# Attention on one Trainium2 core: in each unit, the value products of the previous unit before the first probability transposes instead of behind them

## What is computed

```python
def one_block(args):            # MLA, one block of 128 queries
    ...
    s = jnp.einsum('bqhd,bkhd->bhqk', qi, k).astype(jnp.float32) * scale
    p = masked_softmax(s, kpos[None, :] <= qpos[:, None])
    return jnp.einsum('bhqk,bkhd->bqhd', p.astype(v.dtype), v)
...
    # NSA: three such softmaxes per block, with a bias from the distance, gated and added
    out = gi[..., 0:1] * o_cmp + gi[..., 1:2] * o_slc + gi[..., 2:3] * o_win
```

## Time and profile before

| what | value |
|---|---|
| median of 3 runs | 3,002.99 us (2,997.59 to 3,006.72) |
| the profiled execution | 2,997.87 us, its span 2,996.1 us |
| the attention sweep in it | about 363 to 820 us from the start |
| TensorE, VectorE, ScalarE busy over the whole span | 90%, 38%, 20% |
| DMA | mean 190 GB/s |

### The profile page before, as it was taken

How to read it: one execution, slowest core, us unless ns; L and a number is a source line. 1 busy time by engine, 2 the same in 40 slices (tenths; PEclk the granted TensorE clock), 3 DMA queues, 4 the chain that set the end, 5 groups by cost and what they waited for, 6 DMA issues and landing times.

```text
span 2996.1 us, 41353 instructions
## 1 busy us (share of the span) xinstructions
PE 2693.9 (90%) x12024; PEld 1334.8 (45%) x12025; DVE 1128.5 (38%) x2931; ACT 587.6 (20%) x1583; POOL 219.9 (7%) x187
## 2 busy tenths in 40 slices
PE   6999789999879974999999899999999999899895
PEld 3555466666545641344444343443333344344332
DVE  2676566767636662222222122222222222222221
ACT  1222255555524320001001010010001001000000
POOL 0000000000001111100000101011110100100110
PEclk9999799999989976999999999999999999999998
DMA  8322753030031208767556877587877777755880
GB/s 295 104 63 55 165 152 87 9 95 15 16 99 50 71 36 315 280 224 291 179 185 235 316 284 268 193 317 264 336 294 268 263 264 253 283 191 186 296 297 15
DMA packets 294261, 570.03 MB, mean 190 GB/s; under 512 B 78606, under 2 KB 117262, under 8 KB 273688
## 3 DMA queue, kind: packets, MB, share of 16 engines
q1 hardware_dynamic: 255309, 530.10, 49.5%
q0 software_dynamic: 21152, 38.52, 5.6%
q10 hardware_dynamic: 17707, 0.22, 0.3%
HBM read 542.62 MB, written 69.88 MB: 204 GB/s over the span
## 4 chain that ended last, share of the span: by engine, by line
PE 48%; DMA 6%; issue 3%; DVE 2%; ACTq 1%; ACT 1%; POOL 0%; POOLq 0%; DVEq 0%; SPq 0%
PE ps L1899 27%; PE ps L1991 17%; DMA out<-ys_e,dst 4%; PE ps L2007 2%; DMA wg<-in_w_gate_up 1%; DMA xg<-d_h,src 1%; DVE gu L1801 1%; PE ps L1872 1%; PE ps L1877 1%; ACTq L1614 0%; DVE ys_e L1845 0%; DVE gg L1804 0%; ACT aT L1719 0%; POOL out L1681 0%; DVE ys_e L1843 0%
## 5 line engine op out<-in xcount | busy, mean ns | idle before, releaser
L1899 PE MATMUL ps<-wg,xT_e 128*64 128x512 f32 (+2 forms) x4032 | 1031.0, 599 | 39.2 <-issue 28.2
L1899 PEld LDWEIGHTS ps<-wg,xT_e 128*64 128x64 f32 (+2 forms) x4032 | 390.5, 146 | 649.3 <-issue 649.3
L1991 PE MATMUL ps<-w_rows,aT 128*128 128x512 f32 x1152 | 518.0, 604 | 30.9 <-ACT xT_e L1699 18.6
L1801 DVE TENSOR_TENSOR gu<-ps,bias 64x512 f32<-64x512 f32 (+2 forms) x252 | 173.6, 689 | 587.9 <-PE ps L1899 552.9
L1991 PEld LDWEIGHTS ps<-w_rows,aT 128*128 128x128 f32 x1152 | 217.8, 194 | 288.1 <-issue 288.1
L1741 ACT ACTIVATE ss<-gg 128x256 f32<-128x256 f32 x146 | 60.8, 416 | 1379.8 <-issue 774.1
L1845 DVE TENSOR_SCALAR ys_e<-ps,dst 128x1024 f32<-128x1024 f32 x36 | 46.2, 1284 | 533.8 <-PE ps L1991 533.8
L1681 POOL DMA_INDIRECT out<-ys_e,dst x64 | 101.9, 1592 | 1342.6 <-DVE ys_e L1845 883.7
L804 PE MATMUL ps<-ident_t,sc 128*128 128x128 f32 x880 | 151.1, 288 | 31.3 <-ACT sc L872 27.9
L872 ACT ACTIVATE sc<-sc,nm 128x640 f32<-128x640 f32 (+15 forms) x256 | 161.5, 633 | 60.4 <-DVE nm L914 60.3
L804 PEld LDWEIGHTS ps<-ident_t,sc 128*128 128x128 f32 x880 | 96.7, 142 | 92.0 <-ACT sc L872 64.6
(11 more groups left out here) (319 smaller groups left out, 2479.4 us busy)
## 6 DMA issues: line engine op xcount, KB each, us to landing
wg<-in_w_gate_up SPq DMA_DIRECT2D x128, 2048.0 KB, 8.5
w_rows<-in_w_down SPq DMA_DIRECT2D x128, 1024.0 KB
bias<-in_b_gate_up SPq DMA_DIRECT2D x32, 1024.0 KB
d_bias<-d_rev SPq DMA_DIRECT2D x1, 10368.0 KB, 37.0
w_in<-in_w_in SPq DMA_DIRECT2D x1, 4300.0 KB, 18.3
x_a<-in_x POOLq DMA_DIRECT2D x8, 512.0 KB, 4.0
kn<-d_kn SPq DMA_DIRECT2D x8, 512.0 KB
strip_t<-d_bias SPq DMA_DIRECT2D x8, 512.0 KB
```

What stands on the lines that cost most here:

```text
L1801: read = dve.tensor_tensor(gu[part, :], ps[part, BANK[k][j], :], bias[part, cols], ALU.add)
L1899: mm = pe.matmul(ps[g * kind:(g + 1) * kind, BANK[k][j], :], xT[:, kk, t0:t0 + kind], wg[:, j * groups + g, kk, :], start=(kk == 0), stop= ...
L1991: mm = pe.matmul(ps[:, 2 + 2 * b + h, :], aT[:, j, b * P:(b + 1) * P], wd[:, c, j % 2, h * 512:(h + 1) * 512], start=(j == 0), stop=(j == ...
```

## The change

One call moves up by two places in TensorE's list. `values(u - 1)` now stands ahead of `turn(u, 0)` and `rows_again(u - 2)`; no other engine's list changes, and no instruction is added or removed.

```diff
                 scores(0)
                 scores(1)
                 for u in range(len(UNITS)):
+                    if u:
+                        values(u - 1)
                     turn(u, 0)
                     if u >= 2:
                         rows_again(u - 2)
-                    if u:
-                        values(u - 1)
                     if TURNS[u + 1] - TURNS[u] == 2:
                         turn(u, 1)
                     if u + 2 < len(UNITS):
                         scores(u + 2)
```

## The result

The changed kernel takes 3,087.04 us (median of 4, 3,086.74 to 3,093.4) against 3,004.85 us before (median of 4). The ratio is 1.0288, 95% interval [1.0265, 1.031]: 82 us slower. The forecast had the sign and the place right and the size wrong; its range ended at 3,070.

What follows compares the result with a forecast made beforehand. TensorE's own work was taken to nearly fill the sweep, so its order matters. Per head pair 7.4 + 3.6 + 0.5 + 1.5 - 0.6 = 12.4 us, 49.6 for four, 47 after deductions: forecast 3,047 us, range 3,020 to 3,070.

Steps and rivals of the forecast that it cites:

- V: Big products moved ahead of a small unit's transposes: their time to the next group's start, 1.02 to 1.90 us.
- the first kind: Rounds of m1, m0, c7, c5, w2, where VectorE takes the copy at once: 7.4 us lost per head pair.
- The second kind: Rounds of c6, c3, w1, c4, c1, c2, w0, where VectorE is late for the copy: 3.6 us lost.
- what the chain had to spare: Time transposed tiles lay waiting for VectorE plus the exponential's earliness, taken off the delay; 0.04 + 0.19 us at c5.
- the gain of 0.6: Small products ahead of big transposes fill TensorE's wait at m7 and m6: -0.6 us together per head pair.
- third kind: Places where the next big unit (m3, m2, s3, w3) has only one score part: 0.5 us for the four.
- the forecast's own deduction for the first and the last head pair: 1.9 us hidden in the first pair's existing wait, 0.9 as no m7 follows the last; 2.8 us off.
- the 2.36 us seen there: TensorE's wait for VectorE in the first head pair, where m7's products stand; longest new waits were put below it.
- slower, with the clock: Rival: the clock falls behind the longest new waits, 16 x 3 = 48 us more, 3,095 us; chance 5%.
- faster: Rival: small products fill TensorE's waits before big units' transposes, 24 us less, 2,973 us; chance 5%.
- no change: Rival: the chain's delay and the fuller waits cancel within 9 us, 2,997 to 3,012 us; chance 5%.
- by half: Rival: late-copy places cost nothing and 0.5 us more is spare; 22 us slower, about 3,022 us; chance 15%.

Runs made afterwards that it cites:

- after_filled: The changed kernel plus one 128x512 product of constants into an idle bank ahead of the small products in all 14 small rounds; 3,069.3 us, ratio 1.0241.
- small_first: The changed kernel altered so only the small units' products stand ahead of the next transposes, the big ones behind as before; 3,002.73 us, ratio 1.0023.
- big_first: The changed kernel altered so only the big units' products stand ahead of the next transposes, the small ones behind as before; 3,102.13 us, ratio 1.0355.
- big_half_first: The kernel before with half of each big unit's products ahead of the small unit's transposes, the rest and small products behind; 3,023.49 us, ratio 1.0091.

## Why the prediction was wrong

**Right: what bounds the sweep, and the time of the big products.** V, the time that the moved products take, reads 1.90, 1.68, 1.24 and 1.02 in the new trace as well. With the big products ahead every place but c0 grew by 0.3 us or more, and in the order that the forecast gave: most where VectorE takes the copy at once, less where it is late. Places at the full clock, per head pair: the first kind measured 2.00 + 1.69 + 1.95 + 1.64 + 1.03 = 8.3 (m1, m0, c7, c5, w2). m1 has no undisturbed instance in the changed kernel and is read from `after_filled`, whose filler is shorter than the wait there; so is c6. m0 and c5 have one, in the first head pair. The second kind measured 1.26 (c6) + 0.83 + 0.92 (c3, w1) + 0.52 + 0.74 (c4, c1) + 0.30 + 0.40 (c2, w0) = 5.0. Against these 13.3 us stand 7.4 + 3.6 + 1.5 - 0.6 = 11.9 of the forecast.

The missing 1.4 us are in what the chain had to spare and in the gain. The five places of the first kind lost 8.3 us, and their V is 8.18: nothing was spared there. And the gain of 0.6 that the forecast counted at m7 and m6 is not there: `small_first` has 0.25 more at m1/m6, not less, and w2/m7 lost all of its V.

**Wrong, first step: "Net 0.15. For the four together 0.5 us"** (third kind). I let the small product of s1 move into the wait before m3's transposes and took it off the loss. It cannot start there. It waits for `finish`, which VectorE does behind its copy of s1, which waits for s1's late transposes. It starts at 576.21 and the transposes follow 0.58 later, at 576.79; the first exponential was done at 576.00. Measured: 1.03 (s1), 1.18 (s0), 0.15 (c0), 0.45 (s2), together 2.8 instead of 0.5. `big_first`, where the small products stay behind, loses 2.6 at the same four (0.90, 0.81, 0.40, 0.45), and `small_first` gains nothing at s1 and s0 (0.00 each). So moving the small product gave nothing back. This step makes up 2.3 of the 3.7 us that a head pair loses beyond the forecast.

Together a head pair loses 8.3 + 5.0 + 2.8 = 16.1 us at the full clock where the forecast had 12.4. With the forecast's own deduction for the first and the last head pair that is 4 x 16.1 - 2.8 = 62 us instead of 47.

**Wrong, second step: the clock.** "My longest new waits ... are about 1.5 us each, below the 2.36 us seen there." The waits are somewhat longer (1.8 us ahead of the products of m1, w2 and c6, and 2.0 once at the start), but the comparison with one stretch of the start was the wrong test. The granted clock of the sweep fell from 0.99 to 0.93, a term that the sum put at nothing. Some 26 to 28 us go there by the prices above. The filler checks it: it costs 5.9 us at the short places by itself, two falls that it leaves at w2/m7 cost 2.7, and it bought back 18; together 26.6. The rival "slower, with the clock" named the mechanism and got 5%. That its 3,095 lies only 8 us off is in part luck: it put 16 falls at 3 us, and the sweep had 18 behind its first place, at 1.5 each; what it had too much there, it lacked in the chain. The Trainium skill ("TensorE: Matmul & The Clock Gate", Part 1: The HAM clock gate) says that the rate goes by how busy the engine has been. The trace agrees: the lower level came back in the sweep while TensorE was still busy for 448 of 540 us. I had weighed the rule only by its most visible case.

The two parts give 62 + 28 = 90 us, worked out from one head pair and one place. Read place by place, the profiled sweeps differ by 60.8 us at the full clock and 26.5 us of falls; the first place, where the kernel before has the wait and the fall of the earlier trace rows, is 2.3 us shorter than before, and the opening and closing rounds are 2.3 us longer. That is 87.3 of the 87.4 us (541.3 - 453.9). The medians differ by 82 us: the profiled execution of the kernel before, 2,997.87 us, is 7 us below its median, that of the changed kernel at it.

**The sign marks.** The waits of the transposes did not grow; they passed to the small products ahead of them, so this mark of the forecast was wrong in form, and `big_first` shows it as it was meant. ScalarE's waits for the score maxima fell, 60.3 to 40.0 us, where growth was forecast. The middle head pair took 132 us where 122 was forecast. The places at c5 and c4 moved about as forecast, 1.6 and 0.5 us against "1.3 to 1.5" and 0.4. The rivals faster, no change and "by half" are out. "By half" assumed 0.5 us more to spare; there was less, not more.

**Open.** What exactly tips the clock in one place and not in its twin of the next head pair was not settled. In `after_filled` the wait of 1.80 us ahead of w2's products stands in three head pairs; the clock fell at two of them. Why the chain's spare time was gone at the first kind, and at c7 and m1 even 0.05 and 0.10 us more than V was lost, was not tried either.

## What to carry over

Before moving work forward on an engine that looks full, ask what the instructions behind it release on other engines. Here two short transposes fed a copy, a score part and two exponentials, and 1.7 us of products in front of them arrived almost whole at the other end. A gap that an engine is to fill can be filled only with work whose inputs do not hang on the same chain. And if the move makes one engine wait in every round, its clock is a second cost: price it by the same place with and without a fall.

## What I had not expected of the hardware

One added 128x512 product in each small round made the kernel faster (3,087 to 3,069 us), by holding the granted clock at 0.98. In the changed kernel no wait of TensorE between matmuls of the sweep is as long as the 2.36 us one in the kernel before (the longest is 2.0), and still the sweep came down to 0.93. Past the first three rounds the kernel before has no gap over 0.64 us; the changed kernel has 38 over 1 us. `big_half_first`, whose gaps past these rounds are at most 1.03 us, kept 1.00 there.
